# Attention values for all heads as one seven-block product ahead of the head loop, and rstd rows spread through DRAM

## The chip, the cores and the metric

One core of one Trainium2 chip runs the whole program. The metric is the device time of one execution in microseconds (us). TensorE (PE) multiplies out of SBUF into PSUM, VectorE (DVE) and ScalarE (ACT) do elementwise work, GpSimd (POOL) does elementwise work between SBUF tensors, SyncE (SP) issues most DMAs and ACT some.

## The reference

A decoder of two layers over 1024 tokens and 1024 features, float32. Layer 0's mixer is mLSTM, layer 1's is differential attention; both are followed by a squared-ReLU MLP with 4096 hidden features, and a last RMSNorm ends it. What the change touches:

```
def diff_attention_mixer(u, w_in, lam, norm_g, w_out, layer_idx):
    q, k, v = jnp.split(u @ w_in, 3, axis=-1)          # u = rmsnorm(h, ln_mix[1])
    q = apply_rope(q.reshape(bsz, seq, 8, 2, 64), cos, sin)
    k = apply_rope(k.reshape(bsz, seq, 8, 2, 64), cos, sin)
    v = v.reshape(bsz, seq, 8, 128)
    ...
        s = q_block . k * 64 ** -0.5, causal mask
        p = jax.nn.softmax(s)
        a = p[:, :, 0] - lam_val * p[:, :, 1]
        o = a @ v
    o = rmsnorm(o, norm_g) * (1.0 - lam_init)
    return o.reshape(bsz, seq, D_MODEL) @ w_out
def rmsnorm(x, g): return x * rsqrt(mean(x * x) + EPS) * g
def sq_relu_mlp(u, w_up, w_down): return square(relu(u @ w_up)) @ w_down
```

## The kernel before

**Data and precision.** The residual `h` lies in SBUF with features on partitions: 8 feature tiles of 128 by 1024 tokens. Every large product is made of three matmuls of rounded operands, high by high, low by high and high by low, so each operand is first split: a copy to the high part (ACT, or POOL for weight panels at L618) and a subtraction for the low part (DVE, or POOL at L622).

**Dense panels.** A panel is 128 output features for all tokens: 2 halves of 512 tokens, 8 k steps (units) in each, 3 matmuls of 128x128x512 a unit, so 48 matmuls. `half_panel` (L741 to L743) and `dense` (L759 to L761) issue them into the bank `dps`; DVE's `take` (L1577) scales the result by `rstd_bc`, the row of 1/rms per token repeated on all partitions, and writes `a_next`. SP loads each weight panel into `w_raw`, POOL splits it.

**The MLPs.** Each runs as 8 units (4 chunks, up and down in turn), and each unit is a 1024x1024x1024 product by Strassen-Winograd: 7 block products (stages) in place of 8, each in two half products `q` of 24 matmuls (`half_product`, L859 to L863). POOL forms sums of the stationary blocks (`a_sums`), ACT and DVE split them (`a_split`, `a_rest`) and the moving blocks (`b_split`, `b_rest`), DVE forms the sums of moving blocks (`first_t`, `later_t`) and adds results to `h` (`down_add`). A written order for each engine says what it does at each (stage, q).

**Norms.** Squares are gathered in `acc` while `h` is finished; PE sums them over partitions (`sum_squares`, L767), DVE computes `rstd` with tokens on partitions (`norm`, with a reciprocal square root in steps of 8 elements a partition, L1555 to L1560), and PE spreads it to rows by 8 matmuls with an identity (`broadcast_rstd`, L782), from which DVE copies it to `rstd_bc` (L1571, L1734). In an MLP this stands inside its first unit: sums after half product 0, the spreading after half product 1, and PE waits there for `rstd`.

**Attention.** Each head needs three panels: q, k and v. Panels q0, k0, v0 and q1 come first, straight behind the last down unit (`first_panel` starts on halves of `h` as the last emissions finish them); then head by head the next three panels are fed in units between the attention's own work, at places given by `FEED_AT` (48 units a head, 32 in head 6, none in head 7). ACT swaps rope halves by four DMAs (`swap_halves`, L1438), POOL rotates q and k (`rotate`, L664 to L667), ACT and DVE split them (L1444 to L2062). PE turns the head's values to tokens on partitions by 8 transposes (L1047) and ACT copies them to `vtok`. For each block m of 128 queries: PE computes scores (L1030, L1031), DVE masks the diagonal and takes the maximum (L2073, L2074), ACT exponentiates (L1467), DVE weights the second map and adds it to the first (`combine`, L2081 to L2085), PE transposes the result (L1078), ACT copies it (L1490), PE multiplies by the values (L1084). PE runs one block of scores ahead. At a head's end DVE normalises (L2098, L2101), PE transposes (L1055), and DVE writes the head's output into `h` (L2108); `h` itself was spilled to DRAM (`hspill`) at the start of the attention and comes back for the output product. In head 7 seven eighths of the first output panel are fed between the blocks (`early_tile`), on inputs that POOL splits (`split_early`).

Of the kernel before, what the change touches and what calls it, by code (L numbers as in the profile page):

```python
# [52 lines left out]
FEED_LAST_AT = [(3, 0, 0), (2, 2, 2), (1, 2, 1), (1, 1, 1), (1, 1, 0), (0, 1, 0), (1, 1, 0), (1, 1, 0),  # L53
                (1, 3, 3)]
FEED_LAST = 2 * 16
assert sum(map(sum, FEED_AT[:NB])) < 40
SWAP_AT = [1, 3]
# [47 lines left out]
def trunk(nc, x, ln_mix, ln_mlp, w_up, w_down, ln_f, m_w_in, m_b, m_norm, m_w_out,  # L105
# [8 lines left out]
    G_OUT = [g + 24 for g in G_MIX]  # L114
# [14 lines left out]
    STAGES = 7  # L129
    UP_A = ["a11", "a12u", "s", "s", "a21", "s", "a22u"]  # L130
# [6 lines left out]
    def half_stage(layer, unit, s, q):  # L137

        return 2 * STAGES * UNITS * layer + 2 * stage_of(unit, s) + q + 1

    def read_at(layer, unit, q):

        return 2 * (UNITS * layer + unit) + q + 1
# [10 lines left out]
    def added_at(layer, unit, which, q):  # L154

        return ADDS * (UNITS * layer + unit) + UP_ADDS[which] + q + 1
# [6 lines left out]
    def b_at(layer, unit, s, q):  # L163

        base = B_LAYER * layer
# [9 lines left out]
    def t_at(layer, unit, t, q):  # L175

        return T_LAYER * layer + 8 * ((unit + 1) // 2) + 2 * t + q + 1
# [25 lines left out]
    hspill = nc.dram_tensor("hspill", [P, NT, S], f32, kind="Internal").ap()  # L203
    xs = nc.dram_tensor("xs", [STAGES, P, 2, 4, HALF], f32, kind="Internal").ap()

    with ExitStack() as ctx:
# [6 lines left out]

        h = sb("h", [P, NT, S])
        rstd_bc = sb("rstd_bc", [P, 2, HALF])
        acc = sb("acc", [P, 2, HALF])
        with ExitStack() as s:
            a12d = sb("a12d", [P, 4, HALF], stack=s)
        relu = sb("relu", [P, 2, HALF])
# [14 lines left out]
        with ExitStack() as s:  # L234
            a12u = sb("a12u", [P, 4, HALF], stack=s)
        w_raw = sb("w_raw", [P, 2, NT, P])
# [4 lines left out]
        with ExitStack() as s:  # L241
            fout = sb("fout", [P, NT, D], stack=s)

        def pair_of(first, second, name):
# [4 lines left out]
            return f, g, sb(name, [P, 2, 4, HALF], f32r)  # L249

        a22u, s_blk, hi_high = pair_of("a22u", "s_blk", "one_hi1")
        a21, h11, lo_high = pair_of("a21", "h11", "one_lo1")
        h12, h21, hi_low = pair_of("h12", "h21", "one_hi0")
        h22, a22d, lo_low = pair_of("h22", "a22d", "one_lo0")
        one = ((hi_low, hi_high), (lo_low, lo_high))

# [1907 lines left out]
```

## Time and profile before

| | us |
|---|---|
| median of 3 runs | 2454.58 |
| lowest, highest | 2452.43, 2457.00 |
| the profiled execution | 2454.25 |
| its span in the trace | 2452.5 |
| PE busy | 2307.6 (94%) |
| DVE busy | 1661.5 (68%) |
| POOL busy | 914.1 (37%) |
| ACT busy | 889.7 (36%) |

The profiled execution stands 0.33 us from the median and 1.75 us above its own span. Busy time of PE counts matmuls that overlap, so the pace of PE is better read from the starts of its rows. In the span, the last down unit of layer 0's MLP ends at 1147 us, the first scores stand at 1210.8, and the output of head 7 is written at 1718.

### The profile page before, as it was taken

The numbers are of one execution on the slowest core, as the hardware profiler recorded it, in microseconds if no ns is written. First come the engines' busy times: TensorE is split into PE (matmuls) and PEld (weight loads), VectorE is DVE, ScalarE is ACT, GpSimd is POOL, SyncE is SP. The second block draws the span as 40 slices with busy tenths as digits, with TensorE's granted clock in tenths as the row PEclk, the third lists the DMA queues.
The fourth block names the chain that finished last, engine by engine and source line by source line (L and its number), as shares of the span: only waits on it lengthen the run. The fifth ranks groups of instructions, "written<-read, shape, count | busy, mean of one in ns | idle before, by whom it ended". The sixth has DMA issues, their size and how long they took to land.

```text
span 2452.5 us, 28314 instructions
## 1 busy us (share of the span) xinstructions
PE 2307.6 (94%) x10601; PEld 1899.2 (77%) x10601; DVE 1661.5 (68%) x1956; ACT 889.7 (36%) x1471; POOL 914.1 (37%) x356
## 2 busy tenths in 40 slices
PE   7999997989999999998998999987989999999998
PEld 5788886777888888887777777765777888888887
DVE  7544435579939669398466666666579939669396
ACT  4131122235334243344144444444135334243345
POOL 5424336433423233231644444446433323233230
PEclk9999998999999999999999999999999999999999
DMA  6111111335161542610522222212345271442701
GB/s 175 43 35 34 43 34 52 120 141 220 69 257 69 188 173 69 260 32 19 162 54 59 51 60 60 52 36 76 112 154 206 72 271 59 181 172 73 270 1 69
DMA packets 128832, 262.61 MB, mean 107 GB/s; under 512 B 7217, under 2 KB 81122, under 8 KB 121314
## 3 DMA queue, kind: packets, MB, share of 16 engines
q1 hardware_dynamic: 122658, 243.34, 28.4%
q10 hardware_dynamic: 6080, 17.96, 3.0%
q8 instruction: 65, 1.06, 0.2%
q14 instruction: 29, 0.24, 0.0%
HBM read 202.56 MB, written 41.94 MB: 100 GB/s over the span
## 4 chain that ended last, share of the span: by engine, by line
PE 78%; DVE 11%; issue 3%; ACT 3%; DMA 2%; ACTq 1%; POOL 1%; DVEq 0%; SPq 0%; POOLq 0%
PE aps L859 9%; PE aps L863 9%; PE aps L861 9%; PE dps L759 5%; PE dps L761 5%; PE dps L760 5%; PE dps L863 3%; PE dps L859 3%; PE dps L861 3%; PE mps L863 3%; PE mps L859 3%; PE mps L861 3%; PE dps L741 2%; PE dps L742 2%; PE dps L743 2%
## 5 line engine op out<-in xcount | busy, mean ns | idle before, releaser
L618 POOL TENSOR_TENSOR w_hi<-w_raw,ones 128x1024 fp32r<-128x1024 f32 x64 | 165.9, 2592 | 519.4 <-PE dps L761 290.3
L759 PE MATMUL dps<-one_hi,w_hi 128*128 128x512 f32 x608 | 260.9, 429 | 12.1 <-DVE a_next L1577 12.1
L697 POOL TENSOR_TENSOR s_blk<-s_blk,a 128x1024 f32<-128x1024 f32 x32 | 91.5, 2860 | 443.6 <-DVE w_lo L1621 317.7
L859 PE MATMUL aps<-b_ring,w_hi 128*128 128x512 f32 x640 | 250.0, 391 | 3.0 <-issue 3.0
L863 PE MATMUL aps<-b_ring,w_hi 128*128 128x512 f32 x640 | 249.3, 390 | 0.0
L861 PE MATMUL aps<-b_ring,w_lo 128*128 128x512 f32 x640 | 249.2, 389 | 0.0
L761 PE MATMUL dps<-one_lo,w_hi 128*128 128x512 f32 x608 | 242.8, 399 | 0.0
L760 PE MATMUL dps<-one_hi,w_lo 128*128 128x512 f32 x608 | 242.0, 398 | 0.0
L1639 DVE TENSOR_TENSOR b_ring<-h,b_ring 128x1024 fp32r<-128x1024 f32 x120 | 226.7, 1896 | 7.5 <-ACT b_ring L1242 7.5
L622 POOL TENSOR_TENSOR w_lo<-w_raw,w_hi 128x1024 fp32r<-128x1024 f32 x64 | 160.1, 2501 | 5.0
L859 PE MATMUL aps<-b_ring,a_hi 128*128 128x512 f32 x384 | 151.9, 395 | 9.8 <-DVE b_ring L1639 8.8
L741 PE MATMUL dps<-one_hi,w_hi 128*128 128x512 f32 x384 | 152.5, 397 | 6.9 <-DVE m_next L1577 3.5
L861 PE MATMUL aps<-b_ring,a_lo 128*128 128x512 f32 x384 | 151.2, 394 | 0.0
L743 PE MATMUL dps<-one_lo,w_hi 128*128 128x512 f32 x384 | 151.1, 393 | 0.0
L742 PE MATMUL dps<-one_hi,w_lo 128*128 128x512 f32 x384 | 151.1, 393 | 0.0
L863 PE MATMUL aps<-b_ring,a_hi 128*128 128x512 f32 x384 | 151.0, 393 | 0.0
L859 PEld LDWEIGHTS aps<-b_ring,w_hi 128*128 128x128 f32 x640 | 120.2, 188 | 29.8 <-issue 5.3
L759 PEld LDWEIGHTS dps<-one_hi,w_hi 128*128 128x128 f32 x608 | 117.7, 194 | 32.8 <-DVE a_next L1577 11.1
L863 PEld LDWEIGHTS aps<-b_ring,w_hi 128*128 128x128 f32 x640 | 120.2, 188 | 25.0
L861 PEld LDWEIGHTS aps<-b_ring,w_lo 128*128 128x128 f32 x640 | 120.2, 188 | 24.8
L761 PEld LDWEIGHTS dps<-one_lo,w_hi 128*128 128x128 f32 x608 | 116.6, 192 | 26.3
L760 PEld LDWEIGHTS dps<-one_hi,w_lo 128*128 128x128 f32 x608 | 117.6, 193 | 18.6 <-issue 0.7
(292 smaller groups left out, 5616.8 us busy)
## 6 DMA issues: line engine op xcount, KB each, us to landing
b_ring<-xs SPq DMA_DIRECT2D x42, 2048.0 KB, 7.9
xs<-b_ring SPq DMA_DIRECT2D x14, 2048.0 KB, 7.6
a<-in_w_up SPq DMA_DIRECT2D x16, 1024.0 KB, 5.4
a<-in_w_down SPq DMA_DIRECT2D x16, 1024.0 KB, 7.5
w_raw<-in_mlstm_w_in SPq DMA_DIRECT2D x24, 512.0 KB, 4.0
w_raw<-in_diff_w_in SPq DMA_DIRECT2D x24, 512.0 KB, 3.8
hspill<-h SPq DMA_DIRECT2D x2, 4096.0 KB, 13.3
h<-hspill SPq DMA_DIRECT2D x16, 512.0 KB, 3.6
```

What stands on the lines that cost most here:

```text
L618: nc.gpsimd.tensor_tensor(w_hi[:, slot], w_raw[:, slot], ones[:, :].unsqueeze(1).broadcast_to([P, NT, P]), ALU.mult).then_inc(pool_chain, 1)
L622: nc.gpsimd.tensor_tensor(w_lo[:, slot], w_raw[:, slot], w_hi[:, slot].bitcast(f32), ALU.subtract).then_inc(w_split, 1)
L741: nc.tensor.matmul(dps[:, half], w_hi[:, slot, k], rh, start=(k == 0), stop=False)
L742: nc.tensor.matmul(dps[:, half], w_lo[:, slot, k], rh, start=False, stop=False)
L743: last = nc.tensor.matmul(dps[:, half], w_hi[:, slot, k], rl, start=False, stop=(k == NT - 1))
L759: nc.tensor.matmul(dps[:, half], w_hi[:, slot, k], rh, start=(k == 0), stop=False)
L760: nc.tensor.matmul(dps[:, half], w_lo[:, slot, k], rh, start=False, stop=False)
L761: last = nc.tensor.matmul(dps[:, half], w_hi[:, slot, k], rl, start=False, stop=(k == NT - 1))
L859: nc.tensor.matmul(to[:, n], wh, ring[:, 0, k], start=new and k == 0, stop=False, skip_group_check=not new)
L861: nc.tensor.matmul(to[:, n], wl, ring[:, 0, k], start=False, stop=False, skip_group_check=not new)
L863: last = nc.tensor.matmul(to[:, n], wh, ring[:, 1, k], start=False, stop=(k == 3), skip_group_check=not new)
L1639: last = nc.vector.tensor_tensor(lo, tiles_of(src, q), hi, ALU.subtract)
```

## The change

**Values first.** Behind layer 0's last down unit stands one more unit of seven stages (`V_UNIT`): all eight heads' values as the product of the normed input (without rstd) and `w_v`. Here tokens are the stationary side, so results have tokens on partitions, as the attention wants them, and are scaled by `rstd` per partition as they leave PSUM (`v_copy` on ACT, `v_add` on DVE) into the new tensor `y`. POOL forms the sums of token blocks (`v_sums`), DVE the sums of weight blocks (`v_t`). `h` is spilled to DRAM in four blocks as the down unit finishes them, and ACT scales each block in place by the gain (`scale_x`); near the unit's end ACT and DVE split it into the panels' input (`x_hi_of`, `x_rest`).

**The heads.** Panels are q and k alone: q0, k0 and q1 ahead of the first scores, then two a head (32 units; 16 in head 6), with a shorter `FEED_AT`. Transposes of values and `vtok` are gone. q has two buffers. The head's output goes to `y` instead of `h`, so `h` is reloaded once the last attention panel is done. The head loops are written out.

**rstd rows.** Norms 1, 2 and 3 have no `broadcast_rstd`: SP writes `rstd` to DRAM and reads it back repeated on all partitions, and DVE waits for it (`rows_in`) where it first multiplies by it. In an MLP's first unit PE sums squares after the first 12 matmuls, and waits for `rstd_ready` only at half product 3, for the bank.

**Waits.** Some sums of moving blocks (`first_t`, `later_t`) wait for the split that reads what they overwrite.

```
-FEED_AT = [(2, 0, 0), (2, 3, 2), (2, 2, 2), (1, 2, 2), (1, 2, 2), (0, 2, 1), (1, 2, 1), (1, 2, 1),
-           (1, 3, 4)]
-FEED = 3 * 16
+FEED_AT = [(2, 0, 0), (2, 2, 1), (2, 2, 1), (1, 2, 1), (0, 2, 1), (0, 1, 1), (0, 1, 1), (0, 1, 1),
+           (1, 2, 2)]
+FEED = 2 * 16
-SWAP_AT = [1, 3]
+SWAP_AT = [1, 4]
...
+            def rstd_rows_of(e):
+                sp.wait_ge(rstd_ready, e + 1)
+                sp.dma_start(rstd_rows[e].rearrange("(n p) -> p n", p=P), rstd[:, :],
+                             allow_slow_non_contiguous=True).then_inc(rows_out, 16)
+                sp.wait_ge(rows_out, 16 * e)
+                sp.dma_start(rstd_bc[:, :, :], rstd_rows[e].rearrange("(a b) -> a b", a=2)
+                             .partition_broadcast(P)).then_inc(rows_in, 16)
...
                 if isinstance(g, int) and g in (G_MIX[1], G_MIX[1] + 1):
-                    pool.wait_ge(hs_done, half_stage(0, UNITS - 1, 6, 0) - (1 if slot else 0))
+                    pool.wait_ge(hs_done, half_stage(0, V_UNIT, 6, g - G_MIX[1]))
...
+            def v_sums():
+                pool.wait_ge(x_ready, 2)
+                pool.wait_ge(a_ready, half_stage(0, UNITS - 1, 0, 1))
+                for q in range(2):
+                    nc.gpsimd.tensor_tensor(half_of(xv21, q), half_of(x21, q), half_of(x22, q),
+                                            ALU.add).then_inc(a_added, 1)
...
+            def v_hook(n):
+                if n == 0:
+                    pe.wait_ge(p4_read, read_at(0, UNITS - 1, 1))
+                    sum_squares(2, aps[:, 3])
-                for unit in range(UNITS):
+                for unit in range(UNITS_OF[layer]):
...
-                    pe.wait_ge(oy_out, 2 * hd)
-                pe.wait_ge(evac, 2 * (G_MIX[1] + 3 * hd + 3))
-                for n in range(NB):
-                    last = nc.tensor.transpose(mps[:, n // 4, (n % 4) * P:(n % 4 + 1) * P],
-                                               a_next[:, 2, n * P:(n + 1) * P], ident[:, :])
-                last.then_inc(vt_done, 1)
...
                     for j in range(m + 1):
                         last = nc.tensor.matmul(mps[:, 0, 3 * P:4 * P], at[:, j],
-                                                vtok[:, j], start=(j == 0), stop=(j == m))
+                                                v_all[:, hd, j], start=(j == 0), stop=(j == m))
...
-            first_panel(G_MIX[1], 2)
-            panels(G_MIX[1], G_MIX[1] % 2, 4, *one, skip=1)
+            panels(G_MIX[1], G_MIX[1] % 2, 1, *x_in, x_split, 0)
+            panels(G_MIX[1], G_MIX[1] % 2, 3, *x_in, skip=1)
...
+            def scale_x(b):
+                act.wait_ge(x_spilled[b], 16)
+                for t in range(4):
+                    last = nc.scalar.activation(h[:, d, cut], h[:, d, cut], ACT.Copy,
+                                                scale=gain[:, ROW[2], d:d + 1])
...
+            def v_add(s, q):
+                for p in range(2):
+                    to, n = v_bank(i, f, 2 * q + p)
+                    last = nc.vector.scalar_tensor_tensor(to, bank[:, p].rearrange("p (h d) -> p h d", d=P),
+                                                          rstd[:, n:n + 1], to, ALU.mult, ALU.add)
...
-                dve.wait_ge(spilled, 32)
                 for half in range(2):
-                    nc.vector.tensor_scalar(flat(h[:, ds(hd, 1), half * HALF:(half + 1) * HALF]),
+                    nc.vector.tensor_scalar(y[:, hd, half * HALF:(half + 1) * HALF],
                                             mps[:, half], again[:, 0:1], None, ALU.mult).then_inc(oy_out, 1)
```

How this moves the instructions shows at two places. First PE at the boundary of heads 0 and 1, before: L1055 transposes the finished head's output, L1047 the next head's values, L759 to L761 are a dense unit.

```order
L1055 MATMUL mps<-ident,sq 128x128 x7
L1044 REGISTER_ALU
L1045 ISA [waits oy_out]
L1047 MATMUL mps<-ident,a_next 128x128 [waits evac]
L1047 MATMUL mps<-ident,a_next 128x128 x7
L756 REGISTER_ALU
L757 ISA [waits w_split]
L759 MATMUL dps<-one_hi,w_hi 128x512 [waits evac]
```

The same place after (L1189 is the output's transposes, L880 to L882 a dense unit, L1170 the scores of block 1):

```order
L1189 MATMUL mps<-ident,sq 128x128 x7
L880 MATMUL dps<-one_hi,w_hi 128x512 [waits evac,w_split]
L881 MATMUL dps<-one_hi,w_lo 128x512
L882 MATMUL dps<-x_lo,w_hi 128x512
L880 MATMUL dps<-one_hi,w_hi 128x512
L881 MATMUL dps<-one_hi,w_lo 128x512
L882 MATMUL dps<-x_lo,w_hi 128x512
L1170 MATMUL aps<-k_st,q_hi 128x256 [waits exp_done]
```

The eight value transposes and their two waits (for the head's output and for the value panel's take) no longer stand between the output's transposes and the scores.

Second PE in layer 0's first up unit, before, at the end of half product 1 (L861, L863) and the start of half product 2:

```order
L861 MATMUL aps<-b_ring,w_lo 128x512
L863 MATMUL aps<-b_ring,w_hi 128x512
L782 MATMUL mps<-ident,rstd 128x128 [waits rstd_ready]
L782 MATMUL mps<-ident,rstd 128x128 x7
L859 MATMUL dps<-b_ring,w_hi 128x512 [waits b_ready,a_ready]
```

The same place after:

```order
L993 MATMUL aps<-b_ring,w_lo 128x512
L995 MATMUL aps<-b_ring,w_hi 128x512
L991 MATMUL dps<-b_ring,w_hi 128x512 [waits b_ready,a_ready]
L993 MATMUL dps<-b_ring,w_lo 128x512
L995 MATMUL dps<-b_ring,w_hi 128x512
```

The wait for `rstd` and the eight matmuls that spread it are gone from between the two half products.

## Rows read from the trace of the kernel before

**Rows 1.** Busy time by stretch: PE, PEld, DVE, ACT, POOL, PE clock.

```profile
1147.00:1210.80 63.80, 53.33 (x225) 44.08 (x225) 33.24 (x43) 11.59 (x16) 32.56 (x14) 0.89 0.47 149
...
1272.70:1602.00 329.30, 298.07 (x1580) 247.59 (x1580) 217.72 (x441) 142.85 (x385) 152.35 (x61) 0.96 0.22 56
...
1602.00:1663.50 61.50, 51.20 (x268) 40.82 (x268) 43.84 (x86) 28.54 (x77) 25.14 (x11) 0.94 0.18 43
...
1663.50:1718.00 54.50, 39.75 (x210) 31.31 (x210) 36.15 (x76) 23.35 (x69) 39.22 (x16) 0.92 0.23 68
```

**Rows 2.** PE, first matmuls of half products; DVE, one split: start, length.

```profile
1127.83 1.22 DVE L1621 TENSOR_TENSOR w_lo<-a12d,w_hi 128x1024 fp32r<-128x1024 f32 x1
...
1135.97 0.39 PE L859 MATMUL dps<-b_ring,w_hi 128*128 128x512 f32 x1
...
1141.41 0.39 PE L859 MATMUL mps<-b_ring,a_hi 128*128 128x512 f32 x1
```

**Rows 3.** PE and DVE at the MLPs' starts; idle before in brackets.

```profile
523.86 2.32 DVE L1560 SCALAR_TENSOR_TENSOR rstd<-small,rstd 128x8 f32<-128x8 f32 x1
...
533.13 0.17 DVE L1558 TENSOR_TENSOR small<-rstd 128x8 f32<-128x8 f32 x1
...
533.76 3.78 PE L782 MATMUL mps<-ident,rstd 128*128 128x128 f32 x16 [6.62 <-DVE rstd L1560]
...
1818.80 3.69 PE L782 MATMUL mps<-ident,rstd 128*128 128x128 f32 x16 [6.64 <-DVE rstd L1560]
```

**Rows 4.** DMA issues: size and microseconds to landing.

```profile
h<-hspill SPq DMA_DIRECT2D x16, 512.0 KB, 3.6
...
swap<-a_next ACTq DMA_DIRECT2D x64, 128.0 KB, 2.4
```

**Rows 5.** Timeline of PE between the last down product and the first scores.

```profile
1150.34 0.79 PE L741 MATMUL dps<-one_hi,w_hi 128*128 128x512 f32 x1 [3.33 <-DVE h L1724]
...
1161.24 3.57 PE L767 MATMUL mps<-ones,acc 128*128 128x1 f32 x16 [3.82 <-DVE one_lo L1848]
...
1210.83 0.36 PE L1030 MATMUL aps<-k_st,q_hi 128*128 128x256 f32 x1 [3.35 <-DVE k_st L2062]
```

**Rows 6.** Timeline of DVE and POOL before the first scores.

```profile
1174.87 0.69 DVE L1577 SCALAR_TENSOR_TENSOR a_next<-dps,rstd_bc 128x512 f32<-128x512 f32 x1 [0.75 <-PE dps L743]
...
1182.85 2.39 POOL L664 TENSOR_TENSOR swap<-swap,sinb 128x1024 f32<-128x1024 f32 x1
...
1204.09 6.59 DVE L2062 TENSOR_TENSOR k_st<-a_next,k_st 64x1024 fp32r<-64x1024 f32 x2
```

**Rows 7.** Timeline of DVE: a head's output (L2108), heads 0, 5, 6, 7.

```profile
1272.72 1.41 DVE L2108 TENSOR_SCALAR h<-mps,again 128x512 f32 x2 [2.40 <-PE mps L1055]
...
1601.97 1.41 DVE L2108 TENSOR_SCALAR h<-mps,again 128x512 f32 x2 [2.40 <-PE mps L1055]
...
1663.52 1.41 DVE L2108 TENSOR_SCALAR h<-mps,again 128x512 f32<-128x512 f32 x2 [0.68 <-PE mps L1055]
...
1718.01 1.41 DVE L2108 TENSOR_SCALAR h<-mps,again 128x512 f32<-128x512 f32 x2 [1.87 <-PE mps L1055]
```

**Rows 8.** DVE: weighting of blocks 0, 7 and masks of 1, heads 6, 7.

```profile
1603.85 2.17 DVE L2085 SCALAR_TENSOR_TENSOR ee<-ee,small 128x128 f32<-128x128 f32 x1
...
1610.91 0.30 DVE L2073 TENSOR_TENSOR aps<-aps,mask_qk 128x128 f32<-128x128 f32 x1 [3.70 <-PE aps L1031]
...
1650.58 1.28 DVE L2085 SCALAR_TENSOR_TENSOR ee<-ee,small 128x1024 f32<-128x1024 f32 x1
...
1671.35 0.30 DVE L2073 TENSOR_TENSOR aps<-aps,mask_qk 128x128 f32<-128x128 f32 x1 [2.55 <-PE aps L1031]
...
1706.49 1.28 DVE L2085 SCALAR_TENSOR_TENSOR ee<-ee,small 128x1024 f32<-128x1024 f32 x1
```

**Rows 9.** Timeline of PE: value transposes of heads 6 and 7.

```profile
1603.52 1.09 PE L1047 MATMUL mps<-ident,a_next 128*128 128x128 f32 x8 [1.71 <-DVE h L2108]
...
1668.94 1.94 PE L1047 MATMUL mps<-ident,a_next 128*128 128x128 f32 x8 [5.47 <-DVE a_next L1577]
```

More of the change, by code:

```diff
@@ L446, in six @@
                 def six(i, first=False):
-                    g = G_MIX[layer] + 6 * i
-                    for p in range(6):
+                    g = G_MIX[layer] + (6 if layer == 0 else 4) * i
+                    for p in range(6 if layer == 0 else 4):
                         if layer == 0:
@@ L1173, in split_y @@
                         cut = slice(half * HALF, (half + 1) * HALF)
-                        nc.scalar.activation(piece(one[0], t, half), h[:, t, cut], ACT.Copy).then_inc(ysplit, 1)
+                        nc.scalar.activation(piece(one[0], t, half), Y_AT[layer][:, t, cut],
+                                             ACT.Copy).then_inc(ysplit, 1)
             def emissions(e, g):
@@ new lines, in v_copy @@
+            def v_copy(s, q):
+                i, f, read = {0: (2, 2, p5_read), 1: (1, 1, p1_read), 2: (1, 2, u2_read), 5: (2, 1, p4_read)}[s]
+                act.wait_ge(rstd_ready, 3)
+                act.wait_ge(hs_done, half_stage(0, V_UNIT, s, q))
+                bank = z_bank(q) if s == 0 else x_bank(q)
+                for p in range(2):
+                    to, n = v_bank(i, f, 2 * q + p)
+                    last = nc.scalar.activation(to, bank[:, p].rearrange("p (h d) -> p h d", d=P), ACT.Copy,
+                                                scale=rstd[:, n:n + 1])
+                last.then_inc(read, 1)
@@ new lines, in x_hi_of @@
+            def x_hi_of(b):
+                role, j, _ = ORDER[4 * b]
+                half = tokens(role)
+                cut = slice(half * HALF, (half + 1) * HALF)
+                if b < 2:
+                    act.wait_ge(b_ready, b_at(0, V_UNIT, 3 if b == 1 else 4, 1))
+                else:
+                    act.wait_ge(b_ready, b_at(0, V_UNIT, 1 if b == 3 else 6, 1))
+                for t in range(0, 4, 2):
+                    to = (hi_high if j else hi_low)[:, half, t:t + 2]
+                    nc.scalar.activation(to, h[:, 4 * j + t:4 * j + t + 2, cut], ACT.Copy).then_inc(x_hi, 1)
@@ L1515, in _ @@
             attention_start(0)
-            with act.Fori(0, AH - 1) as hd:
+            for hd in range(AH - 1):
                 attention_core(hd, True)
@@ L1704, in up_relu @@
                 n = read_at(layer, unit, q)
+                if unit == 0 and s == 1:
+                    dve.wait_ge(rows_in, 16 * (2 * layer + 1))
                 if s == 1:
```

575 lines of the change are left out of this document (431 added, 144 removed).

## The prediction, as recorded before the run

> **What bounds the kernel now.** I read the busy time by stretch first [rows 1]. It shows that the stretches the change touches have different limits. The five intervals of heads 1 to 5 take 329.3 us, 65.86 each, with PE near its full load. Head 6, fed two panels instead of three, takes 61.5 us, so sixteen units less (48 matmuls, 10.9 us at PE's pace) bought only 4.4: below three panels a head is set by the chain from masks over exponentials to products, not by PE. Head 7, without panels of its own, still takes 54.5. PE's pace is read from the starts of half products of 24 matmuls [rows 2]: 1135.97 and 1141.41, so 5.44 us each, 0.227 a matmul, without a gap. Next the starts of the two MLPs [rows 3]: PE stands 6.6 us for rstd and then spends 3.8 us in spreading it, once in each layer. Last the way from the last down unit to the first scores [rows 5, 6], and the timelines of the heads [rows 7 to 9]. The sum is made against the profiled execution, 2454.25 us, which is 0.3 below the median of the runs.
>
> **The values' product.** Eight value panels of 48 matmuls go: one ahead of the heads, six in heads 0 to 5, one in head 6. What comes is 14 half products, 14 x 5.44 = 76.2 us, all on the path, since nothing else of PE's can stand there. The stretch from 1147 to the first scores at 1210.8 lasts 63.8 us now: 4 panels, 4 x 48 x 0.227 = 43.5, and 20.3 of gaps, sums and cold matmuls (the clock granted there is 0.89 of full [rows 1]; 3.3 and 3.8 us of idle and 3.6 us of sums [rows 5]). After the change it is made of:
> - the unit, 76.2;
> - its start. The first stationary block needs blocks of h that are final two stages earlier, spilled (1 MB each; 512 KB land in 3.6 us [rows 4]), scaled on ACT and summed on POOL. Put in the written order behind the events of before, it is ready within a microsecond of 1147: 2 us, between 0 and 8;
> - sums of squares inside the unit, 2.5 (3.6 in rows 5 with PE cold);
> - stalls inside the unit: DVE has some 41 splits and sums of 128x1024 at 1.22 [rows 2], 12 results of 128x512 at 0.69 (as the take in rows 6) and 4 us of small things, 62 us of 76, so it fits: 2 us, between 0 and 15;
> - the first panel's split. POOL may write its slot only after half product 12 of 14, and two operations of 2.4 (as in rows 6) follow: 1 us;
> - three panels, 32.7;
> - a wait that the value panel used to fill. From the take of q0 (11.6 us behind the first panel's start) swaps land about 5 us later (2.4 to land [rows 4], behind four issues in a row). From POOL's first rotation at 1182.85 to the first scores at 1210.83 it is 28.0 us in the trace [rows 5, 6]: rotations of q, a split, rotations of k, then ACT's and DVE's split of k, where 6.6 us for two operations show DVE slowed beside POOL. So the scores come 44.6 us behind the panels' start, 12 us behind PE's last panel matmul.
>
> Together 128.4 against 63.8: **+64.6**.
>
> **The heads.** An interval runs from one output to the next [rows 7]. In head 6 it splits into 8.9 us up to block 1's mask, 39.7 up to block 7's weighting and 12.9 to the output [rows 7, 8]; in head 7 into 7.8, 35.1 and 11.5.
> - Up to block 1's mask PE does the value transposes between two waits (1.7 us for the output [rows 9], then for takes) and feeds three units before scores. Without them PE is there in time and DVE's own row of work decides: output 1.4, weighting up to 1606.0, 4.0 behind the output [rows 8], one take 0.7, so 4.7 us instead of 8.9.
> - The middle is DVE's chain with three takes (head 7 has none, head 6 two) and two sets of swap issues on ACT: 38.8, between 35.1 + 2 = 37 and 39.7 + 0.6 = 40.3.
> - The end stays at 12.9.
>
> That makes 56.4 a head. Heads 1 to 5 gain 5 x 9.45 = 47.3. Head 0 (61.9 from the first scores to its output at 1272.72) gains 5.2. Head 6 has one panel, but POOL now splits outputs in it beside DVE: 55.5, gain 6.0. Head 7 loses the 5.5 us wait for the value take [rows 9], of which DVE's own row leaves 3.7, and some POOL work: 4.2. Together **-62.7**. The 64 value transposes and their copies are in these numbers and not counted again.
>
> **The norms.** Removing wait and spreading takes 6.6 + 3.8 = 10.4 us from PE in each layer [rows 3]. But DVE comes out of the norm at the same time as before and is then packed with splits and sums for 30 us; PE catches up with it at stage 3. Following DVE's row of work I give 6 us a layer, **-12** for both, between 0 and 20. The rows must come back from DRAM by DVE's first relu, some 8 us behind rstd. One write of 1024 single elements and one read of 512 KB: not below 2.4 + 3.6 = 6 us by the nearest rows [rows 4], with no row for a write so finely cut. The DRAM trip of the third norm has the whole value unit to hide in. The reload of h at the end of the attention lies beside the last heads, the added waits of DVE are for its own earlier work: nothing.
>
> The Trainium skill speaks against this step: "DMA: Bandwidth & Descriptors", section "Rules for kernel authors", says that a strided last dimension is lowered to one descriptor per element and is to be avoided. No row here shows a transfer of such elements. By that rule the gain of the norms could go whole, which is the second rival below.
>
> **Sum.** 2454.25 + 64.6 - 62.7 - 12 = 2444.1, I take **2444**, 0.4% below. Two large terms nearly cancel, so small errors in either decide the sign.
>
> **Rivals.**
> - *The value unit waits for DVE* (slower). DVE has 62 us of own work in 76, but work beside POOL is stretched: an operation of 8 elements a partition took 2.32 us where its like takes 0.17 [rows 3], and two operations took 6.6 [rows 6]. The unit has six sums of POOL in it, and a split of two operations. If each of the eight costs DVE 1.8 us, DVE reaches 76 us; from there each further microsecond, and each wait for a spill or a scaled block at the start, is PE's. I price it at 1.2 us for each of 14 half products, +17: 2461. For it speaks that the order is new and every engine hands over within a half product; against it, that a down unit of the same size carries the same load without a gap [rows 2].
> - *The rows come late* (within). Then DVE stands at its first relu and the norms give 0 to 3 us: 2455.
> - *The head stays at head 6's time* (slower). If not the value transposes but exponentials and takes set the 8.9 us, heads 1 to 5 stay at 61.5: 5 x 4.4 = 22 in place of 47, and about 8 in place of 15 for the others: 2444 + 32 = 2476. It decides if block 1's masks still stand 8 us or more behind the output.
> - *The heads are faster* (faster). With fewer units in PE's way the middle falls to head 7's 35.1 + 2 and the end to 11.5: 53.3 a head, 3 us less in eight heads, and a value unit without stalls: 2444 - 28 = 2416 at most, about 2430 if half of it comes.
>
> The Trainium skill's "SBUF — State Buffer", section "Terms", has DVE and GpSimd share one port pair which the loser of an arbitration does not get until the other's instruction ends. By that rule the eight POOL operations of the unit block DVE for up to their own 2.4 us each, which is the first rival's mechanism; the 2.32 us operation of the trace agrees.
>
> **How the numbers follow.** Chances: forecast (2436 to 2449) 44%; value unit waits 20%; rows late 14%; heads at head 6's time 7%; faster heads 13%; that the values' product doesn't replace the panels' at all 2%. A measurement of this kernel can tell about 0.2%, 4.9 us, from no change. So faster by more than that 55%, within 22%, slower 23%. The range goes from 2427, half of the fastest case, to 2466, past the price of the first rival: 8 in 10.
>
> **What would show it.** Right: 14 half products at 5.44 us behind 1147 less 6 (norm) with under 5 us of gaps; PE idle some 12 us ahead of the first scores; intervals between outputs of 55 to 58 us; block 1's masks under 5.5 us behind an output; no PE gap in the first up units above 3 us. Wrong: PE waiting on DVE or ACT in the value unit; intervals near 61; DVE waiting for the rows by more than 5 us.

## The result

The changed kernel takes **2475.05 us** (median of 4 runs, 2473.7 to 2475.22) against 2454.42 for the kernel before on the same chip (2452.43 to 2457.0): a ratio of **1.0082**, 95% interval 1.007 to 1.0094. It is slower, by 0.8%. The forecast was 2444 with a range up to 2466, so it was wrong in sign and in range. The profiled execution of after took 2473.7 us, with a span of 2471.9; that of before 2454.25 and 2452.5.

### Where the 19.4 us of span went

| stretch | before | after | difference | forecast |
|---|---|---|---|---|
| first instruction to the first half product of MLP 0 | 514.3 | 511.7 | -2.6 | 0 |
| to the end of MLP 0's last unit | 632.7 | 637.4 | +4.7 | -6 |
| to the first scores | 63.8 | 133.8 | +70.0 | +64.6 |
| first scores to head 7's output | 507.2 | 448.4 | -58.8 | -62.7 |
| to the end | 734.5 | 740.6 | +6.1 | -6 |

The first row is no effect of the change. Before's program, run again with only an addition to attention's head 6 (f4_before_burst below), reached MLP 0 at 511.96, and other executions of the changed program reached it between 511.7 and 515.3: executions differ there by 2 to 4 us.

The first view is the busy time by stretch, as in [rows 1]: length, then busy time of PE, PEld, DVE, ACT, POOL, the granted clock as a share of full, DMA share and GB/s. The stretches are the values' unit, the panels with the wait for scores, head 0, heads 1 to 5, head 6 and head 7.

```profile
1149.10:1238.20 89.10, 82.70 (x353) 67.97 (x353) 68.08 (x67) 49.03 (x61) 22.33 (x8) 0.94 0.11 30
1238.20:1283.00 44.80, 33.53 (x146) 26.93 (x145) 17.74 (x13) 4.23 (x4) 36.03 (x14) 0.91 0.43 118
1283.00:1337.40 54.40, 49.53 (x265) 40.63 (x266) 40.31 (x90) 28.60 (x79) 21.52 (x9) 0.95 0.24 59
1337.40:1603.10 265.70, 237.00 (x1301) 192.60 (x1300) 208.55 (x430) 138.93 (x375) 128.04 (x50) 0.98 0.24 60
1603.10:1680.50 77.40, 40.38 (x214) 32.54 (x214) 66.90 (x85) 27.89 (x75) 53.36 (x20) 0.78 0.31 89
1680.50:1731.30 50.80, 37.91 (x202) 30.02 (x201) 32.96 (x74) 21.90 (x67) 9.58 (x5) 0.86 0.04 11
```

Heads 1 to 5 take 53.1 us each, better than forecast (56.4). Head 6 takes 77.4, where before it took 61.5. It does less PE work than heads 0 to 5 (40.4 us of it, against 47.4 to 49.5) and has the highest share of DVE, 66.9 of 77.4 us, with POOL at 53.4. This one head is 21.9 us above its forecast.

**Head 6.** The timelines of DVE, POOL and PE at its end (start, duration, engine, line, operation, idle before in brackets). L2430 and L2435 split q and k for head 7, L2471 and L1798 to L1803 are the head's rstd, eight numbers a partition, and L753 and L757 split finished heads' outputs for the out product:

```profile
1645.25 6.67 DVE L2430 TENSOR_TENSOR q_lo<-a_next,q_hi 64x1024 fp32r<-64x1024 f32 x2
1651.95 6.53 DVE L2435 TENSOR_TENSOR k_st<-a_next,k_st 64x1024 fp32r<-64x1024 f32 x2
1658.51 2.21 DVE L2471 TENSOR_SCALAR small<-small 128x8 f32<-128x8 f32 x1
1660.76 2.26 DVE L1798 TENSOR_SCALAR small<-small 128x8 int32<-128x8 int32 x1
1663.06 0.17 DVE L1801 TENSOR_TENSOR small<-small 128x8 f32<-128x8 f32 x1
1663.26 2.19 DVE L1802 SCALAR_TENSOR_TENSOR small<-small 128x8 f32<-128x8 f32 x1
```

```profile
1647.50 3.33 POOL L753 TENSOR_TENSOR one_hi<-y,ones 128x1024 fp32r<-128x1024 f32 x1
...
1660.65 2.34 POOL L753 TENSOR_TENSOR one_hi<-y,ones 128x1024 fp32r<-128x1024 f32 x1
1663.07 2.36 POOL L757 TENSOR_TENSOR y_lo<-y,one_hi 128x1024 fp32r<-128x1024 f32 x1
...
1677.25 3.42 POOL L757 TENSOR_TENSOR y_lo<-y,one_hi 128x1024 fp32r<-128x1024 f32 x1
```

```profile
1678.51 1.97 PE L1189 MATMUL mps<-ident,sq 128*128 128x128 f32 x8 [18.74 <-DVE sq L2474]
```

Twelve POOL operations stand back to back from 1647.50 to 1680.67. Of DVE's eleven small operations eight take about 2.2 us and three take 0.17, and PE stands 18.7 us for the product that follows. Each of the eight ends within 0.04 us of the end of a POOL operation (1660.76 + 2.26 = 1663.02 beside 1660.65 + 2.34 = 1662.99): it costs what is left of the operation that POOL has under way. The short ones start where one POOL operation has ended and the next begins (1663.06, POOL 1662.99 and 1663.07). The same chain in the kernel before, and what POOL did behind it:

```profile
1658.33 0.17 DVE L2098 TENSOR_SCALAR small<-small 128x8 f32<-128x8 f32 x1 [0.73 <-ACT acc L1502]
```

```profile
1662.69 2.35 POOL L653 TENSOR_TENSOR one_hi<-h,ones 128x1024 fp32r<-128x1024 f32 x1 [17.83 <-PE dps L761]
```

Before, the splits waited 17.8 us for PE's last panel, the value panel of head 7, and so began 2.2 us behind the end of the chain. The change took that panel away. Its wait was also, written nowhere as such, the gate that kept POOL quiet while DVE finished head 6.

The Trainium skill ("SBUF — State Buffer", section "Terms") says that DVE and GpSimd share a port pair which the loser of an arbitration does not get until the other's instruction ends; the trace agrees: 2.2 us for a small operation of DVE beside POOL operations of 2.3 to 3.4, and the ends above coincide.

**The way to the scores.** PE, as in [rows 5]:

```profile
1152.99 0.79 PE L991 MATMUL dps<-b_ring,w_hi 128*128 128x512 f32 x1 [3.87 <-DVE w_lo L2101]
...
1166.72 1.92 PE L888 MATMUL aps<-ones,acc 128*128 128x1 f32 x16 [2.53 <-DVE acc L2091]
...
1238.24 0.40 PE L862 MATMUL dps<-one_hi,w_hi 128*128 128x512 f32 x1
...
1282.96 0.55 PE L1170 MATMUL aps<-k_st,q_hi 128*128 128x256 f32 x1 [11.27 <-DVE k_st L2435]
```

The values' unit lasts 89.1 us: 76.2 of products, waits of 3.9 and 2.5, 1.8 of sums, and 4.6 lost to matmuls at the lower of the clock's two levels (1.2 GHz of 2.4; granted clock 0.50 from 1153 to 1158), which start 0.43 us apart instead of 0.23: 2.9 behind the first wait and 1.7 behind the sums. No other half product waits.

**The starts of the MLPs.** As in [rows 3], and the two transfers that bring rstd's rows (size, microseconds to landing), as in [rows 4]:

```profile
524.87 2.17 DVE L1798 TENSOR_SCALAR rstd<-small 128x8 int32<-128x8 int32 x1
...
548.45 1.23 DVE L1968 SCALAR_TENSOR_TENSOR h<-h,rstd_bc 128x1024 f32<-128x1024 f32 x1 [3.92 <-DMA rstd_bc<-rstd_rows]
```

```profile
514.64 1.95 PE L888 MATMUL mps<-ones,acc 128*128 128x1 f32 x16
...
533.31 0.47 PE L991 MATMUL mps<-b_ring,a_hi 128*128 128x512 f32 x1 [1.41 <-DVE rstd L1803]
...
543.49 0.77 PE L991 MATMUL dps<-b_ring,w_hi 128*128 128x512 f32 x1 [4.46 <-issue]
...
552.28 0.47 PE L991 MATMUL mps<-b_ring,w_hi 128*128 128x512 f32 x1 [0.99 <-DVE h L1938]
...
561.35 0.63 PE L991 MATMUL aps<-b_ring,a_hi 128*128 128x512 f32 x1 [1.99 <-DVE b_ring L1882]
```

```profile
rstd_bc<-rstd_rows SPq DMA_DIRECT2D x3, 512.0 KB, 5.5
rstd_rows<-rstd SPq DMA_DIRECT2D x3, 4.0 KB, 8.5
```

The one wait of 6.6 us became four, 8.9 us together, and behind the 4.5 us one the granted clock is 0.55 of full (543.49 to 548.40). The round trip takes 14 us by the medians above (15.2 in MLP 0) and DVE stands 3.9 for it. PE's sums came earlier, but DVE's chain came later: it starts 13.0 us behind the MLP's first half product, against 8.8 before, and 12.8 against 8.8 in MLP 1. The sums now stand inside that half product, and it is longer by them and by matmuls at the lower clock behind them (granted clock 0.66 from 516 to 521): it ends 9.2 us behind its start where it ended after 5.4 (7.6 against 5.4 in MLP 1). ACT's split a_hi starts 1.1 us behind that end in both kernels, DVE's a_lo follows it, and the chain stands behind a_lo. From that product to the first matmul of the eighth half product ("seven half products" below) it takes 55.5 us in MLP 0 and 54.1 in MLP 1, against 51.1 and 50.3 before.

### The profile page after: what moved, and what is told of

Its sections match the earlier page's. It is cut to its first block, busy times and chain, and to the rows that moved or that the text cites. A ratio compares the mean times of both kernels' runs of the same rounds, so it can differ in the third digit from the quotient of the medians.

```text
span 2471.9 us, 27055 instructions
## 1 busy us (share of the span) xinstructions
PE 2289.7 (93%) x10441; PEld 1872.1 (76%) x10441; DVE 1718.5 (70%) x1976; ACT 926.2 (37%) x1507; POOL 907.8 (37%) x348
## 4 chain that ended last, share of the span: by engine, by line
PE 72%; DVE 19%; ACT 3%; DMA 3%; issue 3%; POOL 1%; ACTq 0%; SPq 0%; DVEq 0%; POOLq 0%
PE aps L991 10%; PE aps L993 9%; PE aps L995 9%; PE dps L882 3%; PE dps L881 3%; PE dps L880 3%; PE mps L991 3%; PE mps L993 3%; PE mps L995 3%; PE dps L991 3%; PE dps L993 3%; PE dps L995 3%; DVE ee L2458 3%; DVE small L2447 3%; PE dps L862 3%; PE dps L864 3%
## 5 line engine op out<-in xcount | busy, mean ns | idle before, releaser
L717 POOL TENSOR_TENSOR w_hi<-w_raw,ones 128x1024 fp32r<-128x1024 f32 x56 | 139.9, 2499 | 474.6 <-PE dps L882 238.0
L991 PE MATMUL aps<-b_ring,w_hi 128*128 128x512 f32 x680 | 265.7, 391 | 5.2 <-issue 5.2
L995 PE MATMUL aps<-b_ring,w_hi 128*128 128x512 f32 x680 | 265.1, 390 | 0.0
L880 PE MATMUL dps<-one_hi,w_hi 128*128 128x512 f32 x496 | 213.2, 430 | 0.0
L881 PE MATMUL dps<-one_hi,w_lo 128*128 128x512 f32 x496 | 196.1, 395 | 0.0
L991 PE MATMUL aps<-b_ring,a_hi 128*128 128x512 f32 x408 | 163.5, 401 | 12.9 <-DVE b_ring L1882 11.9
L995 PE MATMUL aps<-b_ring,a_hi 128*128 128x512 f32 x408 | 161.8, 397 | 0.0
L862 PE MATMUL dps<-one_hi,w_hi 128*128 128x512 f32 x368 | 144.3, 392 | 3.5 <-DVE m_next L1820 3.5
L863 PE MATMUL dps<-one_hi,w_lo 128*128 128x512 f32 x368 | 144.0, 391 | 0.0
L1377 ACT ACTIVATE b_ring<-h 128x1024 fp32r<-128x1024 f32 x112 | 116.4, 1047 | 45.4 <-DVE h L1925 37.5
L991 PE MATMUL dps<-b_ring,w_hi 128*128 128x512 f32 x304 | 121.5, 400 | 11.5 <-issue 7.6
L1405 ACT ACTIVATE h<-h 128x1024 f32<-128x1024 f32 x64 | 67.8, 1060 | 160.2 <-DVE h L1968 157.1
L1864 DVE TENSOR_TENSOR w_lo<-s_blk,w_hi 128x1024 fp32r<-128x1024 f32 x68 | 88.0, 1294 | 55.6 <-ACT w_hi L1343 55.6
L1343 ACT ACTIVATE w_hi<-s_blk 128x1024 fp32r<-128x1024 f32 x68 | 71.9, 1057 | 142.0 <-PE aps L995 104.3
```

The source lines that it names most:

```text
L717: nc.gpsimd.tensor_tensor(w_hi[:, slot], w_raw[:, slot], ones[:, :].unsqueeze(1).broadcast_to([P, NT, P]), ALU.mult).then_inc(pool_chain, 1)
L862: nc.tensor.matmul(dps[:, half], w_hi[:, slot, k], rh, start=(k == 0), stop=False)
L863: nc.tensor.matmul(dps[:, half], w_lo[:, slot, k], rh, start=False, stop=False)
L880: nc.tensor.matmul(dps[:, half], w_hi[:, slot, k], rh, start=(k == 0), stop=False)
L881: nc.tensor.matmul(dps[:, half], w_lo[:, slot, k], rh, start=False, stop=False)
L991: nc.tensor.matmul(to[:, n], wh, ring[:, 0, k], start=new and k == 0, stop=False, skip_group_check=not new)
```

## Experiments

Times are medians of 4 to 10 runs; the kernel before had medians of 2454.3 to 2455.5 beside them.

### Is it POOL's splits that lengthen head 6?

**e1_hold**, after with

```diff
                 pool.wait_ge(half_done, 2 * G_OUT[layer])
+                if layer == 1:
+                    pool.wait_ge(oy_out, 2 * (AH - 1))
```

> The changed kernel with one wait more: GpSimd splits the outputs of the finished heads for the out product only once head 6's output has been written, where the trace of the kernel before shows that work. Theory A (the burst of twelve 128x1024 operations on GpSimd, 1647.5 to 1680, stretches VectorE's chain of 8-element operations at the end of head 6): head 6's interval falls from 77.4 us to 52 to 56, the chain from 18.7 to 2 to 4, head 7 gives back 3 to 5 of it (before, with the splits in head 7, it took 54.5 against 50.8 now), and the kernel takes 2453 to 2459. Rival B (head 6 is long because TensorE has one panel instead of two to fill it, or because its q_lo copy is late, and GpSimd only happens to be busy): head 6 stays at 70 to 78 and the time at 2470 to 2480.

Measured 2458.59 (ratio to before 1.0014, 1.0005 to 1.0024): 16.5 less than after. Head 6 takes 56.5 (0.5 over the expected range), head 7 54.8 (50.8 in after: it has the splits now). DVE's chain, and POOL's first split:

```profile
1653.68 0.17 DVE L2473 TENSOR_SCALAR small<-small 128x8 f32<-128x8 f32 x1 [0.69 <-ACT acc L1747]
```

```profile
1662.42 2.34 POOL L755 TENSOR_TENSOR one_hi<-y,ones 128x1024 fp32r<-128x1024 f32 x1 [14.23 <-issue]
```

All eleven small operations take 0.17. Theory A holds and B falls.

**f1_hold_half**, after with a hold for the later outputs alone:

```diff
-                        pool.wait_ge(oy_out, 2 * (t + 1))
+                        pool.wait_ge(oy_out, 2 * (t + 1) if t < 3 else 2 * (AH - 1))
```

> The changed kernel, with GpSimd's splits for the out product of heads 0 to 2 left where the change puts them (from 1647 us on) and those of heads 3 to 6 held until head 6's output is written. Theory A (the loss of head 6 grows with the number of GpSimd operations that run beside VectorE's small ones): six operations of 2.3 to 3.4 us end near 1667 instead of 1680; the chain of head 6 starts late (about 1658.5, since q_lo and k_st are still stretched) and four or so of its twelve operations take 2.2 us instead of eight: head 6's interval 66 to 70 us, between 56.5 with all held and 77.4 with none, and the time 2463 to 2469. Rival B (some other wait of head 6 went with the hold): 2458 or 2475, not between.

Measured 2463.10 (1.0038, 1.0025 to 1.005), head 6 66.8: between, as A has it. Three small operations take 2.2 us and eight 0.17; the last long one starts before POOL's sixth operation ends (1667.49) and ends with it, all behind it are short:

```profile
1665.32 2.19 DVE L1802 SCALAR_TENSOR_TENSOR small<-small 128x8 f32<-128x8 f32 x1
1667.55 0.17 DVE L1803 SCALAR_TENSOR_TENSOR small<-small 128x8 f32<-128x8 f32 x1
```

**f4_before_burst**, the kernel before with work added to POOL that nobody reads:

```diff
                 split(g, 1, (g + 1) // 2)
+                for n in range(8 if layer == 1 else 0):
+                    if n > 0:
+                        pool.wait_ge(idle_n, n)
+                    nc.gpsimd.tensor_tensor(swap[:, 1].rearrange("p (a b) -> p a b", b=P),
+                                            swap[:, 1].rearrange("p (a b) -> p a b", b=P),
+                                            ones[:, :].unsqueeze(1).broadcast_to([P, NT, P]),
+                                            ALU.mult).then_inc(idle_n, 1)
                 split_early(layer)
```

> The kernel before with eight GpSimd operations more, 128x1024 in float32 like the splits, one behind the other from the end of the out panel's split (1644.9) in head 6; nobody reads what they write. They cover the end of head 6, and put off the real splits by some 6 us. Theory A: VectorE's chain of 8-element operations (1658.33 to 1660.55 before) has four or more of 2.2 us, its q_lo and k_st operations take 3.3 instead of 1.2, and head 6's interval is 70 to 76 instead of 61.5: 2462 to 2470 in all. Rival B (it is something of the new layout, the separate tile of outputs or the single panel, and not GpSimd's work as such): 2453 to 2457.

Measured 2467.84 (1.0058, 1.0041 to 1.0075), head 6 74.9 instead of 61.5. POOL's eight operations and DVE beside them:

```profile
1642.62 24.61 POOL L717 TENSOR_TENSOR swap<-swap,ones 128x1024 f32<-128x1024 f32 x8
```

```profile
1651.70 6.70 DVE L2065 TENSOR_TENSOR q_lo<-a_next,q_hi 64x1024 fp32r<-64x1024 f32 x2
1658.43 6.57 DVE L2070 TENSOR_TENSOR k_st<-a_next,k_st 64x1024 fp32r<-64x1024 f32 x2
1665.04 2.23 DVE L2106 TENSOR_SCALAR small<-small 128x8 f32<-128x8 f32 x1
```

The q and k splits are stretched from 1.2 to 3.3 us each, the same as in after (6.67 and 6.53 for two), in a kernel that has nothing of the change. So it is POOL's work as such, not the new layout. Here only two small operations were long, against four or more expected: the burst ended 2 us behind the chain's start, and most of head 6's 13.4 us came through q, k (8.4 us together) and the weighting ahead of them (3.4 us instead of 1.3).

### Does the norm lose by the way through DRAM, or by DVE's queue?

**e2_norm_first**, after with DVE's norm ahead of its split of A's fourth half block:

```diff
+                        if c == s == 0 and q == 1:
+                            mlp_norm(layer)
                         a_rest(layer, unit, 2 * s + q + 2)
...
                 elif (s, q) == (0, 1):
-                    mlp_norm(layer)
                     first_t(layer, 0, 1)
```

> The changed kernel, but at the start of each MLP VectorE takes the sums and works out rstd ahead of its share of the fourth A split (half stage (1, 1)) instead of behind it. Theory C (the earlier sums bring nothing because VectorE's rstd chain is queued behind the a_lo split, which waits for ScalarE's a_hi, which waits for the end of the first half product; the way through DRAM then starts too late): the chain starts 518 to 520 instead of 524.68, the waits of TensorE at 533.31 and 543.49 (1.41 and 4.46 us) and VectorE's 3.92 us wait for the broadcast rows go, and each MLP start is 4 to 7 us shorter: 2461 to 2467. Rival D (the way through DRAM itself is the loss, whenever it starts, or the a_lo split that now comes later makes TensorE wait as long): under 2 us per layer, 2471 to 2477.

Measured 2463.55 (1.0036, 1.002 to 1.0051), 11.5 less than after. The chain runs from 519.03 to 521.21, each operation 0.17, and DVE no longer waits for the rows. But its row of work behind it:

```profile
521.04 0.17 DVE L1803 SCALAR_TENSOR_TENSOR rstd<-small,rstd 128x8 f32<-128x8 f32 x1
...
524.98 5.69 DVE L1898 SCALAR_TENSOR_TENSOR h<-h,gains,a22d 128x512 f32<-128x512 f32 x2
530.59 3.43 DVE L1879 SCALAR_TENSOR_TENSOR b_ring<-h,b_ring 128x1024 fp32r<-128x1024 f32 x1
```

```profile
540.97 0.55 PE L991 MATMUL dps<-b_ring,w_hi 128*128 128x512 f32 x1 [3.30 <-issue]
```

The same two groups took 1.29 and 1.22 us in after, where they came once POOL's sums were done. POOL's sums run at this place either way; what DVE does beside them is stretched, and PE waits for it at the fifth half product. Seven half products take 50.9 us in MLP 0 and 48.9 in MLP 1. Theory C is right on the size of the gain, but of the two waits of PE only the first went; the second shrank from 4.46 to 3.30.

**e3_pe_broadcast**, after with the rows of the MLP norms by TensorE as before (in short; `mlp_rstd` is that of before):

```diff
-                rstd_rows_of(2 * layer + 1)
...
+                        if unit == s == 0:
+                            broadcast_rstd(e, mps)
...
+                    mlp_rstd(layer)
```

> The changed kernel with the rstd rows of the two MLP norms made by sixteen TensorE products again (as before), the sums left at their new, earlier place; the values' norm still goes through DRAM. Theory C: the chain still starts behind the a_lo split, so TensorE waits about 7 us for rstd (before: 6.62) and then pays 3.4 for the products, but VectorE no longer reads late rows: each MLP start 51 to 53 us instead of 55.5 and 54.1, the kernel 2467 to 2473. Rival D (the DRAM way is the loss and the early sums are worth their 5 us): each start 45 to 48, the kernel 2456 to 2462.

Measured 2466.28 (1.0046, 1.0029 to 1.0062), 0.7 under C's range and far from D's.

```profile
525.01 0.15 DVE L1812 TENSOR_SCALAR small<-mps 128x8 f32<-128x8 f32 x1
```

```profile
533.41 3.78 PE L903 MATMUL mps<-ident,rstd 128*128 128x128 f32 x16 [6.46 <-DVE rstd L1805]
```

With the sums 5 us earlier PE waits 6.46 us for rstd, as it did before (6.62): the early sums bring nothing, since the chain is queued behind the a_lo split, whose a_hi waits for the end of the first half product (DVE stood 4.25 us for it). They even cost: with TensorE's rows as before, seven half products take 52.7 and 51.7 us, against 51.1 and 50.3 before. Issued so late, the way through DRAM costs 8.8 us more than TensorE's rows do.

**f3_before_norm_first**, the kernel before with the same reordering as e2:

> The kernel before, with one edit: in the first unit of each MLP VectorE works out rstd ahead of the a_lo split of half stage (1, 1). Nothing else of the change is in it, the sums stay behind the first half product. Theory C (the 6.62 us that TensorE waits for rstd come from where the chain stands in VectorE's queue, ahead of four of its operations being stretched to 2.3 us beside GpSimd): the chain starts about 521.5 instead of 523.05 and takes 2.2 us instead of 10.5, the two waits go, and part of each comes back as VectorE is the engine that is late next: 2442 to 2449. Rival F (VectorE is the bound of this stretch in any order): 2451 to 2456.

Measured 2454.09 (0.9999, 0.9989 to 1.0009): no difference, so rival F holds and C's 2442 to 2449 missed.

```profile
520.39 0.17 DVE L1560 SCALAR_TENSOR_TENSOR rstd<-small,rstd 128x8 f32<-128x8 f32 x1
520.59 2.27 DVE L1558 TENSOR_TENSOR small<-rstd 128x8 f32<-128x8 f32 x1
```

```profile
527.54 2.72 PE L782 MATMUL mps<-ident,rstd 128*128 128x128 f32 x11 [3.02 <-DVE rstd L1560]
```

POOL's first sum starts at 520.43, and from there the chain is slow. PE's wait is halved to 3.0 us, yet seven half products take 49.1 us in MLP 0 (51.1 before) and 49.1 in MLP 1 (50.3): PE meets DVE again at a b_ring split (1.7 us).

**g2_rows_by_pe**, f2 (below) with TensorE's rows, which prices the DRAM way where it is issued early:

> f2_value_sums_later with the rstd rows of the two MLP norms made by TensorE as before instead of the way through DRAM; the rstd chain still runs first, beside nothing of GpSimd's. This prices the way through DRAM by itself, where it is issued early. If it is then off the path (14 us from 521 on, against a reader at 542), TensorE's sixteen products (3.4 us) and VectorE's copy (1.2 us) come back in each layer: 2446 to 2452. Rival D (the rows' transfers delay other loads or the reader, so that they cost as much as TensorE's products): 2441 to 2445.

Measured 2441.78 (0.9944, 0.9929 to 0.9959) against 2443.51 for f2. The forecast of 2446 to 2452 missed, and the time lies in rival D's range: TensorE's rows cost no more than DRAM's. Two things were mis-sized. In the kernel before, the sixteen products stood behind a wait and ran at the lower clock (granted clock 0.50, 3.4 us from their start to the next product's); here they follow at once at the full clock and take 1.7. And what they take comes off PE's later waits for DVE, 3.7 and 4.9 us in g2's two layers, 5.6 and 5.9 in f2's. Seven half products take 49.7 and 49.9 us in g2, 49.2 and 49.3 in f2, so by the traces the products cost half a microsecond a layer. D's own reason, that the rows' transfers delay others, is not shown. The products and the wait behind them in g2:

```profile
526.57 1.95 PE L905 MATMUL mps<-ident,rstd 128*128 128x128 f32 x16
```

```profile
537.72 0.63 PE L993 MATMUL mps<-b_ring,a_hi 128*128 128x512 f32 x1 [3.73 <-DVE acc L1990]
```

### The values' unit

**f2_value_sums_later**, e4 (below) with the sums at the end of the second half product:

```diff
                 def v_hook(n):
-                    if n == 0:
+                    if n == 1:
```

> e4_hold_norm with one edit more: TensorE makes the sums of the values' norm at the end of the second half product of the values' unit instead of its middle. In the trace of e4_hold_norm it waits there 3.65 us for VectorE's last addition to acc, and the next eight products run at the lower clock. If that wait is on the path to the first scores, it goes: 2443 to 2446. Rival E (rstd is then late for the evacuation of the first banks, which VectorE and ScalarE scale by it, and TensorE waits in the fourth half product instead): 2447 to 2451.

Measured 2443.51 (0.9961, 0.9948 to 0.9973) against 2447.84 for e4. PE waits 0.33 us for acc instead of 3.65, and the chain is hardly late (a wait of 0.26 us for rstd): the wait was on the path. The intervals of the two kernels overlap a little (e4: 0.9961 to 0.998), so the 4.3 us do not stand by the times alone; in the traces the way from the unit's first product to the first scores falls from 131.6 to 126.2 us.

**g1_value_split_first**, f2 with the unit's first split ahead of two squares on ACT and DVE:

```diff
                 for n in range(*at):
+                    if layer == 0 and n == 12:
+                        v_a_split(0)
                     last_emit(layer, n)
...
-                    v_a_split(0)
                     scale_x(2)
```

That is ACT's half of the edit; DVE's does the same with `v_a_rest(0)`.

> f2_value_sums_later with one edit more: at the end of the MLP's last unit ScalarE and VectorE split the first operand of the values' unit (its first half) ahead of the last two squares and additions to acc instead of behind them. In the trace of f2 TensorE waits 3.85 us there for that split, and its next eight products run at the lower clock (0.43 us apart instead of 0.23); GpSimd's sum that the split reads had ended about 1141.7, and ScalarE waited 5.43 us for acc meanwhile. If the order in the queues is the cause: 2438 to 2441. Rival G (VectorE is busy without a gap there, and beside GpSimd, so that the second half product or the sums wait instead): 2442 to 2446.

Measured 2443.07 (0.9952, 0.9938 to 0.9965), the same as f2: rival G. PE's first wait falls to 2.1 us, and the wait for acc is back:

```profile
1145.60 0.50 PE L993 MATMUL dps<-b_ring,w_hi 128*128 128x512 f32 x1 [2.06 <-DVE w_lo L2105]
...
1160.21 1.92 PE L890 MATMUL aps<-ones,acc 128*128 128x1 f32 x16 [3.22 <-DVE acc L2095]
```

DVE is without a gap but 0.5 us from 1136 to 1161; the order there only chooses where PE waits for it.

### Do the parts add?

**e4_hold_norm**, both edits of e1 and e2:

> Both edits together, GpSimd's splits held and rstd worked out first. By theories A and C the two gains lie in different stages and add: 2442 to 2450, which would be faster than the kernel before (2454). If the clock or a later stage gives one of them back: 2455 to 2462.

Measured 2447.84 (0.997, 0.9961 to 0.998). The edits gave 16.5 and 11.5 alone and 27.2 together: two separate losses.

**g3_values_hold**, e3 with e1's hold, that is the values' part alone:

> The values' part of the change alone, with GpSimd's splits held: rows of the MLP norms by TensorE and rstd behind the a_lo split, as in the kernel before (only the sums stay early, which e3_pe_broadcast showed to bring nothing). The gains found so far add if they lie in separate stages: e3's 2466.3 less the hold's 16.5, 2448 to 2452, so that the values' part by itself would be worth 3 to 7 us against before. If the values' part is worth nothing without the norms' part: 2453 to 2458.

Measured 2448.98 (0.9973, 0.9963 to 0.9983). The values' product first is worth 5.9 us by itself, once POOL is held. The early sums are still in this kernel, and seven half products take 52.3 and 53.5 us in it against 51.1 and 50.3 before, so without them it may be worth some 4 us more; no run shows that.

**h1_hold_panel_too**, g2 with the hold moved ahead of the split of the first out panel:

```diff
                 g = G_OUT[layer]
+                if layer == 1:
+                    pool.wait_ge(oy_out, 2 * (AH - 1))
                 split(g, 1, (g + 1) // 2)
```

> g2_rows_by_pe with the hold one step earlier on GpSimd: the split of the out product's first panel (2.34 and 3.22 us in head 6, beside VectorE's last ee weighting of 3.2 and its q_lo operations of 4.6 us together, where TensorE waits 6.4 us for q_lo against 2.1 in head 5) waits for head 6's output too. Theory A (what is left of head 6 above the others, 58.9 against 53, is the same contention): head 6 falls to 54 to 57; the splits behind end 5.6 us later, which head 7's early products give back in part: 2438 to 2442. Rival H (the early products of head 7 now come late, since they need that panel first): head 7 grows by as much or more, 2442 to 2447.

Measured 2438.01 (0.9927, 0.9913 to 0.9942), the fastest of all and 0.7% under before. PE's wait for q_lo fell from 6.4 to 2.4 us and head 6 from 58.9 to 55.9, but head 7 rose from 52.8 to 55.4. Theory A's mechanism is there; that the exchange pays is not shown, since the profiled executions of g2 and h1 have the same span (2440.3 and 2441.3) and the intervals of the ratios overlap.

## Why the prediction was wrong

The profiled execution of after lies 29.5 us above the forecast (+19.4 where -10.1 was forecast), by these steps:

- **Heads 1 to 5: right mechanism, too small.** "56.4 a head" measured 53.1, about the number of the rival *the heads are faster* (53.3), which shortened the middle (37.1) but the end as well (11.5), and the end did not shrink. The three parts were 4.7, 38.8 and 12.9; they measure 4.4, 34.9 and 13.8 in the mean of the five heads. So the middle was mis-sized: it takes what head 7's took without any panel (35.1), and takes and swaps add nothing to it. Gain over forecast 16.2 us. Head 0 took 54.4 for 56.7, head 7 50.8 for 50.3.
- **Head 6: the first step that failed.** The forecast says: "Head 6 has one panel, but POOL now splits outputs in it beside DVE: 55.5, gain 6.0." The new overlap was seen and named, but no term stands for it: 55.5 is 0.9 below a head with two panels, though the same text has two operations at 6.6 us beside POOL and an 8-element one at 2.32. It took 77.4: +21.9. The right working: from 1647.5 on POOL has twelve operations in a row, and DVE has four splits and eleven small operations, each of which can cost about 2 us more, the rest of a POOL operation. e1 takes POOL away and 16.5 us go; f4 puts POOL's work into before, and the time grows by 13.0. What was not asked: the splits' old gate was a value panel, and the change removes it.
- **The norms: the second step that failed, and as large. "-12 for both" was +10.8** (+4.7 and +6.1, the second with all that follows head 7). Three assumptions fell. That DVE "comes out of the norm at the same time as before" was meant as harmless; relative to PE it came 4.2 us later, since the early sums lengthened the half product that the chain waits for (MLP 0 in after; e3 has the same start). The round trip was bounded from below only, by 6 us, and took 14, against the 8 that it had (the rival *rows come late* had the mechanism, but gave it no loss). And the 10.4 us taken from PE (10.1 from the wait's start to the next product) were gained in none of the orders tried, since DVE is late next, at the fourth, fifth or seventh half product: seven half products take 49.7 and 49.9 us in g2, 49.2 and 49.3 in f2 and 49.1 twice in f3, against 51.1 and 50.3. Off by 22.8 us in the sum.
- **The way to the scores: +64.6 was +70.0.** The unit took 89.1 where the terms gave 82.7: its start 3.9 for 2, and the clock, for which no term stood, 4.6. "Stalls inside" (2) and the sums (2.5) were 2.5 and 1.8. The likeliest rival, *the value unit waits for DVE*, occurred only at the unit's start and at the sums, 6.4 us of waits and not 17: half products 3 to 14 follow at 5.4 to 5.5 us. The panels and the wait behind them took 44.8 for 45.7.
- Executions differ: -2.6 in the stretch that the change leaves alone.

Together -16.2 - 2.3 + 21.9 + 0.5 + 22.8 + 5.4 - 2.6 = 29.5.

So 2475 came near the price of *the head stays at head 6's time* (2476) by chance: the heads did not stay there, and heads 1 to 5 ran at the time of the opposite rival.

The Trainium skill ("DMA: Bandwidth & Descriptors", section "Rules for kernel authors") says that a strided last dimension is lowered to one descriptor per element. The trace agrees as far as it goes: the 4 KB of rstd needed 8.5 us, while 512 KB came back in 5.5. But avoiding the transfer gains nothing over issuing it early (g2 against f2).

What stays open: what the values' part is worth without the early sums, and whether h1's last step pays.

## What to carry over

When a piece of work is removed, look for who waited for it: here a wait for a value panel was the only thing that kept POOL's big operations off a chain of small DVE ones, and one explicit wait in its place was worth 16.5 us. Price an overlap of POOL and DVE by the number of DVE instructions in it and not by their length: each can wait for the end of the POOL operation under way, here about 2 us whatever its own size. And a result computed earlier on one engine helps nobody while the next step stands behind another wait in its engine's queue; look where DVE's row of work ends before counting PE's wait as a gain, and look who waits for the work that the earlier step now delays.

## What the runs showed of the hardware

- VectorE beside back-to-back GpSimd operations of 128x1024 float32 (2.3 to 3.4 us each): an 8-element operation 2.2 us instead of 0.17, a 64x1024 split 3.3 instead of 1.2. The GpSimd operations are slowed as well: of the twelve in after's head 6 those beside the q and k splits take 3.2 to 3.3 us, those beside the small operations 2.3 to 2.4. The long small operations end within 0.04 us of the end of a GpSimd operation, in after, f1 and f4 alike. Not every small operation is caught: of eleven, eight in after, three in f1, two in f4.
- Sixteen 128x128 matmuls took 3.8 us behind a wait of 6.6 us (before, granted clock 0.50) and 1.95 without a wait (g2, granted clock 1.00); to the start of the next product it is 3.4 and 1.7. So a step's price read behind a wait holds only together with that wait.
- 4 KB written to DRAM as 1024 single elements landed after 8.5 us, 512 KB read back as a broadcast after 5.5 (medians of three in after).
